# The last output product of a two-block network, by token instead of by feature, with its residual turned on the way

## The reference

```python
def hybrid_layer(x, ...):
    h = rmsnorm_2(x, norm_w)
    proj = jnp.matmul(h, w_in)                 # 1024 -> 4360 columns
    ...                                        # attention, retention, mLSTM: ya, yb, yc
    y = jnp.concatenate([ya, yb, yc], axis=-1)
    return x + jnp.matmul(y, w_out)            # 1024 -> 1024, added to the residual x

def second_block(x, ...):
    for layer in range(DEPTH_2):               # 2
        x = hybrid_layer(x, ...)
    return rmsnorm_2(x, final_norm_w)          # x * rsqrt(mean(x*x) + 1e-6) * w
```

## Time and profile before

| | |
|---|---|
| time, median of 3 runs (lowest to highest) | 908.88 us (908.74 to 909.06) |
| the profiled execution, its own time | 909.29 us |
| its span, first to last instruction | 908.0 us |
| busy: TensorE, VectorE, ScalarE | 863.3 us, 413.7 us, 301.3 us |
| mean granted TensorE clock | 0.988 of full speed |

### The profile page before, as it was taken

One profiled execution on the slowest core, in us unless ns is written; L12 is line 12 of the kernel. 1 busy time (PEld: TensorE's weight loads), 2 busy tenths in 40 slices (PEclk: granted clock), 3 DMA queues, 4 the chain that ended last, 5 costly groups with the idle time before them and its releaser, 6 DMA issues.

```text
span 908.0 us, 12408 instructions
## 1 busy us (share of the span) xinstructions
PE 863.3 (95%) x5152; PEld 561.8 (62%) x5152; DVE 413.7 (46%) x802; ACT 301.3 (33%) x544; POOL 10.3 (1%) x14
## 2 busy tenths in 40 slices
PE   5999999999998989898999899999999999999997
PEld 3668875334444434442444243498878999887997
DVE  3196954111210202111111011189798887898973
ACT  4253142111111101110111011165646676537572
POOL 0001000000000000000000000000100000000000
PEclk9999999999999999999999999999999999999999
DMA  9999989999999999999999999864414444432431
GB/s 373 424 428 427 398 350 416 397 430 427 427 427 429 428 427 425 427 427 429 428 427 428 427 424 420 340 236 183 140 47 186 147 162 190 176 140 94 143 138 47
DMA packets 26266, 291.40 MB, mean 321 GB/s; under 512 B 2912, under 2 KB 3424, under 8 KB 4320
## 3 DMA queue, kind: packets, MB, share of 16 engines
q1 hardware_dynamic: 26208, 290.58, 77.6%
HBM read 289.52 MB, written 1.05 MB: 320 GB/s over the span
## 4 chain that ended last, share of the span: by engine, by line
PE 72%; DMA 22%; DVE 4%; issue 1%; ACT 0%; SPq 0%
PE bank L1446 22%; PE bank L1019 16%; DMA ring<-in_expert_w 11%; DMA more<-in_expert_w 10%; PE bank L1050 8%; PE bank L1470 5%; PE bank L403 3%; PE bank L950 2%; PE bank L419 2%; DVE X L373 2%; PE bank L990 2%; DMA ring<-in_ada_w 2%; PE bank L446 2%; PE bank L1620 1%; PE bank L1494 1%; PE bank L1646 1%
## 5 line engine op out<-in xcount | busy, mean ns | idle before, releaser
L1019 PE MATMUL bank<-ring,xg 128*64 128x512 f32 x760 | 233.3, 605 | 14.1 <-DMA ring<-in_expert_w 14.1
L1446 PE MATMUL bank<-HH,halves 128*128 128x256 f32 x848 | 164.1, 289 | 0.0
L1019 PEld LDWEIGHTS bank<-ring,xg 128*64 128x64 f32 x760 | 73.2, 139 | 134.5 <-issue 108.7
L1446 PEld LDWEIGHTS bank<-HH,halves 128*128 128x128 f32 x848 | 135.5, 193 | 5.6 <-issue 4.8
L1019 PE MATMUL bank<-more,xg 128*64 128x512 f32 x256 | 118.6, 615 | 6.7 <-DMA more<-in_expert_w 6.7
L1446 PE MATMUL bank<-HL,halves 128*128 128x256 f32 x424 | 120.4, 284 | 0.0
L1050 PE MATMUL bank<-ring,X 128*64 128x512 f32 x384 | 114.3, 596 | 0.7 <-ACT X L1090 0.7
L1137 DVE TENSOR_TENSOR X<-X,bank 128x512 f32<-128x512 f32 x16 | 11.0, 688 | 227.2 <-PE bank L1019 227.2
L1347 DVE TENSOR_TENSOR halves<-raw,halves 128x1024 fp32r<-128x1024 f32 (+1 forms) x84 | 92.1, 1129 | 6.3 <-ACT halves L1339 6.2
L1150 DVE SCALAR_TENSOR_TENSOR ygL<-bank,small,ygH 128x512 fp32r<-128x512 f32 x32 | 24.0, 751 | 136.1 <-ACT ygH L1097 136.1
L1446 PEld LDWEIGHTS bank<-HL,halves 128*128 128x128 f32 x424 | 81.7, 193 | 0.8 <-issue 0.5
(11 more groups left out here) (347 smaller groups left out, 1201.9 us busy)
## 6 DMA issues: line engine op xcount, KB each, us to landing
ring<-in_expert_w SPq DMA_DIRECT2D x63, 2048.0 KB, 26.8
more<-in_expert_w SPq DMA_DIRECT2D x22, 2048.0 KB, 26.1
raw<-in_units SPq DMA_DIRECT2D x38, 1024.0 KB, 4.8
ring<-in_ada_w SPq DMA_DIRECT2D x10, 2048.0 KB, 20.9
ring<-in_expert_w SPq DMA_DIRECT2D x17, 1024.0 KB, 28.1
ring<-in_w_in SPq DMA_DIRECT2D x3, 2048.0 KB, 34.8
more<-in_ada_w SPq DMA_DIRECT2D x2, 2048.0 KB, 27.9
ring<-in_w_out SPq DMA_DIRECT2D x2, 2048.0 KB, 21.8
```

Source lines behind the costliest of these rows:

```text
L1019: t = pe.matmul(bank[3 + i][64 * x:64 * x + 64, :], xg[q % 2][:, k, o + 64 * x:o + 64 * x + 64], w[:, k, :], start=k == 0, stop=k == 7)
L1446: t = pe.matmul(ps[:, T * j:T * j + T], part(x[:, k, 128 * j:128 * j + 128]), part(y[:, k, :]), start=first and a == 0, stop=last and a == ...
```

## The change

The output units of layer 1 are made by token. The activations (`YH`, `YL`) are stationary and 512 columns of weights move in each product: 96 products of 512 columns take the place of 192 of 256. Units 18 and 19 are made together for both halves j of the tokens, then units 20 and 21 for tokens 0 to 127, then for tokens 128 to 255. The residual must lie by token for this. VectorE turns `xT` in blocks of 32x32 into `yT` (`turn_squares`, four instructions, placed behind `low(1, 3)` and ahead of `rows_of_scale`), and 16 transfers, issued by SP in twos behind the loads of units 6 to 13 of layer 1, put the blocks in place in `xT`, now by token (`xtok`). Each moves 32 partitions x 16 x 32 numbers, 64 KB in runs of 128 bytes. The final norm works by token: its weight comes as a row (`fnr`, a new input of 512 KB, loaded into `raw[0]` when units 18 and 19 are done), the squares are summed by ScalarE's accumulator, and the reciprocal root is a column that VectorE and ScalarE multiply by. TensorE has nothing to do after its last output product. The host turns the output differently.

```diff
             def second_sp():
...
+                    if MOVING <= U < MOVING + 8:
+                        sp.wait_ge(s_turn, 16)
+                        for a in range(4):
+                            if a // 2 == (U - MOVING) % 2:
+                                b = (U - MOVING) // 2
+                                sp.dma_start(squares_to(a, b), squares_from(a, b)).then_inc(s_tok, 16)
+                sp.wait_ge(s_unit, 2 * NU - 2)
+                sp.dma_start(fn_row, p["fnr"]).then_inc(s_ring[0], 16)
+                for j in range(2):
+                    sp.wait_ge(s_od, j + 1)
+                    sp.dma_start(out[:, j, 512:1024], ytok[:, j, 512:1024]).then_inc(s_out, 16)
+                    sp.wait_ge(s_fin, j + 3)
+                    sp.dma_start(out[:, j, 0:512], ytok[:, j, 0:512]).then_inc(s_out, 16)
...
+                def out_by_token(u, order, halves_of, ready):
+                    at = (NU + u) % 4
+                    ps = {j: start(1, u + j) for j in halves_of}
+                    for i, k in enumerate(order):
+                        if halves_of[0] == 0:
+                            pe.wait_ge(*ready(k))
+                            if i % 4 == 0:
+                                pe.wait_ge(*made(1, u, k))
+                                pe.wait_ge(*made(1, u + 1, k))
+                        wl, wh = (halves[:, at:at + 2, x, T * k:T * k + T] for x in range(2))
+                        for j in halves_of:
+                            for a, (x, y) in enumerate(((YH, wh), (YH, wl), (YL, wh))):
+                                t = pe.matmul(v3(ps[j][:, :], 2), part(x[:, k, 128 * j:128 * j + 128]), part(y), ...)
+                    t.then_inc(s_unit, len(halves_of))
...
-                stats(1, s_sqx, 16, (0, 1))
-                stats(1, s_sqy, 8, (6,))
-                stats(1, s_sqy, 9, (7,))
-                for _ in range(8):
-                    pe.matmul(bank[5][:, 0:T], part(YH[:, 0, 0:128]), part(YH[:, 0, :]), start=True, stop=True)
-                spread_pe(14, 0)
...
                     for i in range(4):            # ScalarE, layer 1
+                            j, f = i % 2, i // 2
+                            act.wait_ge(s_xo, 5 + i)
+                            act.activation(flat(squares[:, 2 * i:2 * i + 2, :]), xtok[:, j, 512 * f:512 * f + 512], ACT.Square,
+                                           accum_out=sums2[:, j, f:f + 1]).then_inc(s_sqy, 1)
+                            if f:
+                                act.wait_ge(s_rs, 14)
+                                act.wait_ge(s_sqy, 5 + i)
+                                act.activation(root[:, j:j + 1], sums2[:, j, 1:2], ACT.Sqrt, bias=rest[:, j:j + 1],
+                                               scale=1 / 1024).then_inc(s_rt2, 1)
+                                act.wait_ge(s_rs, 15 + j)
+                                act.activation(ytok[:, j, 0:512], ytok[:, j, 0:512], ACT.Copy, scale=rcol[:, j:j + 1]).then_inc(s_fin, 1)
...
+                def turn_squares():
+                    for k in range(0, 8, 2):
+                        dve.transpose(turned[:, k:k + 2, :, :], xT[:, k:k + 2, :].rearrange("p k (h n) -> p k h n", h=2)).then_inc(s_turn, 1)
+                def residual_tok(i):
+                    j, f = i % 2, i // 2
+                    dve.wait_ge(s_unit, (NU + 20, NU + 20, NU + 21, NU + 22)[i])
+                    ...
+                    dve.tensor_tensor(at, unit_bank(1, U_OUT + (0, 1, 2, 3)[i])[:, :], at, ALU.add).then_inc(s_xo, 1)
+                def weigh_tok(i):                 # i == 0 waits for fn_row
+                    dve.tensor_tensor(ytok[...], xtok[...], fn_row[:, 512 * f:512 * f + 512], ALU.mult).then_inc(s_xs, 1)
+                def rest_tok(j):
+                    dve.tensor_scalar(rest[:, j:j + 1], sums2[:, j, 0:1], 1 / 1024, 1e-6, ALU.mult, ALU.add).then_inc(s_rs, 1)
+                def scale_tok(j):
+                    dve.wait_ge(s_rt2, 4 + j)
+                    dve.reciprocal(rcol[:, j:j + 1], root[:, j:j + 1]).then_inc(s_rs, 1)
+                    dve.tensor_scalar(ytok[:, j, 512:1024], ytok[:, j, 512:1024], rcol[:, j:j + 1], None, ALU.mult).then_inc(s_od, 1)
```

More of the change, by code:

```diff
@@ L1474, in by_token @@
                         yield
+                def out_by_token(u, order, halves_of, ready):
[10 more added lines that the diff above has]
+                            for a, (x, y) in enumerate(((YH, wh), (YH, wl), (YL, wh))):
+                                t = pe.matmul(v3(ps[j][:, :], 2), part(x[:, k, 128 * j:128 * j + 128]), part(y), start=i == 0 and a == 0,
+                                              stop=i == 7 and a == 2, skip_group_check=True)
+                    t.then_inc(s_unit, len(halves_of))
                 def pair(l, u, order, piece, ready):
@@ L1739, in second_pe @@
                     late = (6, 7, 4, 5, 0, 1, 2, 3)
[L1740 to L1744, removed]
                     if l:
-                        pe.wait_ge(s_xo, 6)
-                        tile(l, 21, 1, late, bank[4])
-                    else:
-                        tile(l, 21, 1, late)
-                stats(1, s_sqx, 16, (0, 1))
-                stats(1, s_sqy, 8, (6,))
-                stats(1, s_sqy, 9, (7,))
-                for _ in range(8):
-                    pe.matmul(bank[5][:, 0:T], part(YH[:, 0, 0:128]), part(YH[:, 0, :]), start=True, stop=True)
-                spread_pe(14, 0)
+                        out_by_token(U_OUT, late, (0, 1), y_ready(l))
+                        out_by_token(U_OUT + 2, late, (0,), y_ready(l))
+                        out_by_token(U_OUT + 2, late, (1,), y_ready(l))
+                    else:
+                        both = pair(l, U_OUT, late, 4, y_ready(l))
+                        take(both, 8)
+                        tile(l, 20, 0, late)
+                        tile(l, 20, 1, late)
+                        tile(l, 21, 0, late)
+                        tile(l, 21, 1, late)
             def second_act():
@@ L2326, in second_dve @@
                     low(l, 21)
-                    for i in range(4):
-                        if l and i == 3:
-                            residual_end()
-                        else:
+                    if l == 0:
+                        for i in range(4):
                             residual(l, i)
-                        if l and i in (1, 2):
-                            add_squares(l, i)
-                        if l == 0:
                             x_low(1, 2 * i)
@@ L2340, in second_dve @@
                                 add_squares(l, i)
-                dve.wait_ge(s_rt2, 4)
-                dve.reciprocal(rcol, root).then_inc(s_rs, 1)
-                on_diagonals(rcol, 13)
-                dve.wait_ge(s_rcT, 4)
-                for i in range(4):
-                    dve.wait_ge(s_fin, 2 * i + 4)
-                    dve.tensor_tensor(yT[:, 2 * i:2 * i + 2, :], yT[:, 2 * i:2 * i + 2, :],
-                                      bank[6][:, 0:T].unsqueeze(1).broadcast_to([128, 2, T]), ALU.mult).then_inc(s_od, 1)
+                residual_tok(0)
+                residual_tok(1)
+                weigh_tok(0)
+                weigh_tok(1)
+                rest_tok(0)
+                rest_tok(1)
+                residual_tok(2)
+                weigh_tok(2)
+                scale_tok(0)
+                residual_tok(3)
+                weigh_tok(3)
+                scale_tok(1)
             return second_sp, second_pe, second_act, second_pool, second_dve, residual_act, residual_dve, again
@@ L2507 @@
     got = r.results[0]["out_0"]
-    return np.ascontiguousarray(got.transpose(2, 1, 0).reshape(1, 256, 1024))
+    return np.ascontiguousarray(got.transpose(1, 0, 2).reshape(1, 256, 1024))
```

58 lines of the change are left out of this document (35 added, 23 removed).

## The result

The changed kernel takes 905.62 us at the median of 12 runs (903.95 to 908.5), against 908.82 us for the kernel before in 12 runs beside it (907.5 to 912.16). The ratio is 0.9962, with a 95% interval of 0.995 to 0.9975: 3.4 us faster, and 2.3 to 4.5 by the interval. The forecast was 904.6, 4.2 us faster. The profiled execution took 905.45 us.

A forecast was written before the change was run, and what follows sets the result against it. TensorE was taken as the chain throughout layer 1, plus 8.96 us after its last product. Span 908.0 − 1.1 − 3.1 = 903.8 us, other costs 0; median time forecast 904.6, own range 904.0 to 905.6, reaching up to 907.2.

The forecast's parts named there:

- the weight's row: Final weight's row, loaded after units 18 and 19: VectorE's work behind it ends at 894.7, covered by 3.2 us.
- Products: Layer 1's output units: 96 products at 0.2273 us replace 192 at 0.120, ending at 897.96 instead of 899.04; gain 1.08 us.
- the wait for the second pieces of units 18 and 19: First pair of output units, k = 0: TensorE waits because both units' second pieces are asked for at once; counted 0.15 us.
- What follows the last product: Final norm and stores after TensorE's last output product: 5.8 us instead of 8.96, gain 3.1 us.
- last store lands: End of the kernel: the second 256 KB store, issued at 901.07, takes 2.7 us and lands at 903.8.
- it does not gain at its end: Rival, last stage: 0.3 us more at each of six handovers, gain 2.4, time 906.5; chance 0.04.
- The turn: Four VectorE transposes ahead of the copy into `rs`: 0.69 us each, 2.8 together, cost 0.
- cover: VectorE's 2.69 us idle before the copy into `rs` plus 0.8 after the gate chain: up to 3.5 us free.
- slow transposes: Rival, ahead of `stabilisers`: 1.4 us per transpose, four take 5.6, 2.1 over what is free; time 906.7, chance 0.07.
- the sign turn at 7.7 us of transposes: Ahead of `stabilisers`: four transposes totalling 3.5 + 4.2 = 7.7 us would cancel the gain; above that, slower, chance 0.02.
- The transfers: Sixteen 64 KB transfers behind loads of units 6 to 13: 0.5 to 1 us of queue each, no loss up to 2.3.
- the forecast's slack: ScalarE behind unit 11's load: 2.8 us of idle ahead of 806.90 to absorb a late load.

## Why the prediction was right, and what was mis-sized

**The mechanism and the sign were right.** The stream of products and the chain behind it were both shortened by what replaced them, and neither the turn, nor its transfers, nor the weight's row cost anything on the chain.

*Products.* Forecast: first start at 875.83, last end at 897.96, a gain of 1.08 us. Measured: 875.63 and 897.97, a gain of 0.87. That the two ends agree is luck: this trace came to the stage 0.20 us early, and the stream took 0.21 more than forecast. Of this, 0.17 is the wait for the second pieces of units 18 and 19. The chain shows only 0.08 of idle there, but the three products from 880.88 on take 881.88 − 880.88 = 1.00 us, where three steps of 0.2273 are 0.68: 0.32 where I counted 0.15. Making the products narrow again gives back 0.9 us, all of the gain.

*What follows the last product* is the term that was mis-sized most: 6.2 us and not 5.8, so its gain was 2.7 and not 3.1. By its own steps, forecast and measured ends:

| step | forecast | measured |
|---|---|---|
| VectorE's addition | 898.69 | 898.69 |
| square and accumulator | 899.55 | 899.44 |
| root | 899.85 | 900.11 |
| reciprocal | 900.06 | 900.31 |
| ScalarE's half scaled | 900.73 | 901.05 |
| last store lands | 903.8 | 904.2 |

The root comes 0.26 late, because of the 0.35 us gap that I had no term for; in its absence (the kernel with the waits swapped) that step would have been ahead of the forecast. ScalarE's multiplication by a column is 0.72 and not 0.63. I took 0.63 from a square, which has no operand on the partitions. The last store's issue starts at 901.22, where I had 901.07: I had left 0.34 us between the scaled half and this issue, so only 0.15 of the delay remains there. And the store lands 3.0 us behind its issue's start, against 2.7, which adds 0.28 and is the larger part of the miss. The median of the four stores is 2.7, but the last of them is the one that counts.

The rival "it does not gain at its end" had named this place, but priced it as six handovers at 0.3 more each; there was one such gap, and the others were 0.02.

*The turn.* Forecast: 4 × 0.69 = 2.8 us in a cover of 3.5. Measured: 2.48 us, and without any turn the chain is the same to 0.01 us. Twelve transposes, 7.54 us, overran the cover by the 4.0 us that the rows had promised (7.54 − 3.5). So the cover, and with it the rival *slow transposes*, was priced rightly, except that in that kernel TensorE's wait also came with 1.5 us of lower clock. The prediction has the sign turn at 7.7 us of transposes; at 7.54 the kernel was already 0.2% slower than before.

*The transfers.* Forecast: 0.5 to 1 us of queue each, and a loss only above 2.3. Measured: 1.26 to 2.17 for a pair on SP's queue, mostly 1.26, and 0.78 and 0.81 each in the two rows of sixteen, where the issuing sets the pace. The Trainium skill (VectorE: DVE Perf Modes, The three transpose paths) says that a plain DMA which transposes through its access pattern is 19 times slower than the DMA's own transposing path, which I had read as an estimated 2.9 us on these 64 KB. No run here has such a transfer: VectorE had turned the elements, 128 bytes are contiguous, and SP was held for at most 1.1 us each (the pair of 2.17). The margin was wider than I had worked out, too. Moving all of them to the place that I held to be tight changed nothing.

In one small thing the forecast's model was wrong. It had the transfers delay only later loads, and not the load that they follow. Unit 11's load, is waited for 2.61 us instead of 2.10,

```profile
802.39 2.01 ACT L1353 ACTIVATE halves<-raw 128x1024 fp32r<-128x1024 f32 x2 [2.61 <-DMA raw<-in_units]
806.70 0.39 ACT L1833 ACTIVATE scr<-bank 128x256 f32<-128x256 f32 x1 [2.31 <-PE bank L1608]
```

and its issue is not late (796.96). Its own two transfers move beside it: in the seven other traces that have them there the wait is 2.37 to 3.00 us, in the three that have none there it is 2.07 to 2.17. The idle time behind it shrinks by the same 0.5 us (2.81 to 2.31), as the forecast's slack had it, and the chain does not notice.

*The time itself.* 905.6 against 904.6, at the upper edge of the forecast's own range: 0.4 us of this is the end and 0.2 the products. For the remaining 0.4 no cause can be named, as the runs of the changed kernel spread over 4.5 us (903.95 to 908.5).

## What to carry to other kernels

Where a stage ends a kernel, count what stands behind its last product step by step: here a layout in which the sum of squares lies along the free dimension took three visits to TensorE and three quarters of the last scaling out of the end, and was worth about three times what the wider products were (2.7 and 0.9 us; what each of its parts is worth was not tried apart). Work that only prepares such a layout can be put for nothing where an engine idles, as long as its length is compared with the idle time *and* with the slack of the next reader; once it overruns, TensorE pays the overrun and perhaps its clock. Where an engine on the chain waits for two semaphores, try asking first for the one that comes last: at the two roots where it was tried, it took away 0.35 and 0.06 us.

## What the runs showed of the hardware that was not expected

- At ScalarE's last root, a satisfied semaphore wait ahead of the late one came with 0.37 us of idle, and in the other order with 0.03; at two other roots the first order came with only 0.09.
- Sixteen transfers of 64 KB in runs of 128 bytes were limited by SP's issuing, 0.78 us each on average (0.63 at the median), against 0.33 for most loads of 1 MB. They landed 2.3 and 2.9 us after issue (medians) in the two kernels that issued them in a row, and 5.5 in pairs behind a load.
- A transpose of 128x512 float32 in 32x32 blocks on VectorE took 0.62 to 0.63 us in a row of several (2.48 for four, 7.54 for twelve), less than an addition of that shape reading PSUM (0.69).
- After three stops of 1.80, 0.95 and 1.22 us, TensorE's granted clock fell to 0.50 at about 789 us and was 1.00 again at 793, and 24 products took 4.36 us instead of 3.06.
